# Softmax sums of an attention stage: two engines' halves joined by VectorE and summed one pair of steps later

## The reference, cut to what matters

```python
def mla_attention(q, ckv, kpe, w_kvb, w_o):          # 8 heads; scale = 96 ** -0.5
    ...
    def block(q_blk):
        s = (jnp.einsum('bqhd,bkhd->bhqk', q_blk[..., :QK_NOPE], k_nope)
             + jnp.einsum('bqhr,bkr->bhqk', q_blk[..., QK_NOPE:], kpe))
        p = jax.nn.softmax(s.astype(jnp.float32) * scale, axis=-1).astype(v.dtype)
        return jnp.einsum('bhqk,bkhd->bqhd', p, v)
    ...
    return o @ w_o
```

## Time and profile before

| | us |
|---|---|
| median of 3 runs | 3183.33 |
| lowest and highest | 3180.16 and 3183.79 |
| the profiled execution, its device time | 3184.42 |
| the profiled execution, its span | 3182.6 |

### The profile page before, as it was taken

How to read it: one execution, slowest core, us unless ns; L and a number is a source line. 1 busy time by engine, 2 the same in 40 slices (tenths; PEclk the granted TensorE clock), 3 DMA queues, 4 the chain that set the end, 5 groups by cost and what they waited for, 6 DMA issues and landing times. The chain is left out here.

```text
span 3182.6 us, 43970 instructions
## 1 busy us (share of the span) xinstructions
PE 2928.4 (92%) x16924; PEld 2348.9 (74%) x16924; DVE 1934.8 (61%) x2561; ACT 1084.9 (34%) x1718; POOL 1061.3 (33%) x686
## 2 busy tenths in 40 slices
PE   6999999999789999999999979979954999999993
PEld 2888888888667777777777757768834888888882
DVE  4418393839347777777777746545674555555565
ACT  4411111111344444444444423213422344343434
POOL 0000000000123343444333535421214766666652
PEclk8999999999889999999999999989976999999996
DMA  5312222211540101110110136574414566666667
GB/s 210 109 54 105 76 105 80 105 64 67 177 140 10 27 19 26 25 33 13 27 25 6 60 94 205 173 242 163 158 54 141 184 199 204 202 212 200 207 187 281
DMA packets 139524, 371.26 MB, mean 117 GB/s; under 512 B 20886, under 2 KB 47996, under 8 KB 129116
## 3 DMA queue, kind: packets, MB, share of 16 engines
q1 hardware_dynamic: 99820, 266.47, 25.3%
q0 software_dynamic: 23984, 74.71, 8.3%
q10 hardware_dynamic: 15552, 27.79, 2.5%
HBM read 265.99 MB, written 102.89 MB: 116 GB/s over the span
## 5 line engine op out<-in xcount | busy, mean ns | idle before, releaser
L1160 ACT ACTIVATE at_w<-at_sc 128x512 f32<-128x512 f32 (+1 forms) x592 | 346.3, 591 | 417.8 <-PE at_sc L1235 362.8
L1322 DVE TENSOR_REDUCE at_mpart<-at_mx 128x2 f32<-128x512 f32 x575 | 368.5, 683 | 167.0 <-PE at_mx L1262 166.9
L1210 POOL TENSOR_TENSOR at_part<-at_part,at_w 128x512 f32<-128x512 f32 x224 | 297.4, 1328 | 359.4 <-ACT at_w L1160 356.1
L2479 POOL TENSOR_TENSOR moe_gu_lo<-moe_raw_gu,moe_gu_hi 128x2048 fp32r<-128x2048 f32 x64 | 296.6, 4635 | 121.7 <-ACT moe_gu_hi L2545 121.3
L520 DVE SCALAR_TENSOR_TENSOR fr_r<-fr_r,fr_dw 128x2334 f32<-128x2334 f32 x120 | 318.0, 2650 | 3.9
L377 PE MATMUL fr_po<-hT_hi,fr_w_hi 128*128 128x512 f32 (+1 forms) x800 | 297.1, 371 | 3.1 <-PE fr_po L377 1.9
L377 PE MATMUL fr_po<-hT_hi,fr_w_lo 128*128 128x512 f32 (+1 forms) x800 | 294.7, 368 | 0.0
L377 PE MATMUL fr_po<-hT_lo,fr_w_hi 128*128 128x512 f32 (+1 forms) x800 | 294.6, 368 | 0.0
L1274 PE MATMUL at_acc<-at_w,V 128*64 128x256 f32 (+1 forms) x2368 | 289.7, 384 | 0.0
L2664 DVE TENSOR_TENSOR moe_d_lo<-moe_raw_d,moe_d_hi 128x1024 fp32r<-128x1024 f32 x64 | 184.1, 2876 | 105.3 <-ACT moe_d_hi L2576 105.3
L1349 DVE TENSOR_TENSOR at_part<-at_part,at_w 128x512 f32<-128x512 f32 x224 | 228.9, 1022 | 19.7 <-ACT at_w L1160 6.7
(11 more groups left out here) (391 smaller groups left out, 6800.5 us busy)
## 6 DMA issues: line engine op xcount, KB each, us to landing
moe_raw_gu<-w_gate_up SPq DMA_DIRECT2D x64, 1024.0 KB, 4.8
moe_raw_d<-w_down SPq DMA_DIRECT2D x64, 512.0 KB, 5.2
fr_wm<-w_ada_rows POOLq DMA_DIRECT2D x32, 512.0 KB, 4.1
gates_scratch<-fr_r ACTq DMA_DIRECT2D x64, 256.0 KB, 2.0
mx_gates<-gates_scratch SPq DMA_DIRECT2D x64, 256.0 KB, 3.1
fr_raw<-w_in SPq DMA_DIRECT2D x28, 512.0 KB, 5.1
fr_r<-x POOLq DMA_DIRECT2D x18, 512.0 KB, 4.6
raw<-mixed_scratch SPq DMA_DIRECT2D x9, 1024.0 KB, 6.2
```

The source lines that it names most:

```text
L1160: act.activation(w[:, g % NW, k, 0:n], sc[:, (2 * g + k) % SCB, 0:n], ACT.Exp, scale=SM_SCALE).then_inc(exp_done, 1)
L1210: pool.tensor_tensor(part[:, j % 2, 1, 0:n], before, w[:, g % NW, 1, 0:n], ALU.add).then_inc(add_p, 1)
L1322: dve.tensor_reduce(mpart[:, s, 2 * half:2 * half + 2, c], max_bank(m, half), AX.X, ALU.max).then_inc(red_done, 1)
L2479: pool.tensor_tensor(gu_lo[:, slot], raw_gu[:, slot], gu_hi[:, slot].bitcast(F32), ALU.subtract).then_inc(glo_done, 1)
```

## The change

On every block's end DVE gets one more instruction, `join(j)` (line 1362 of the changed kernel): it adds POOL's partial sum to its own, in place. It waits for both running sums. In DVE's list it stands at the end of the pair in which the block's last `add` is. PE then makes only two products with ones, from the joined sum (`sum_up`), instead of four. They are no longer issued behind the block's last `values` but in the next pair: for b3 between the first `max_products` and the second `scores` of that pair, for all other blocks right ahead of its `values`. ACT's `take_out` moves with them: b3's stands behind the exponentials of the first step of that next pair, those of the others behind the second step's. DVE's `divide` of the last head moves by one pair too. POOL's and SP's lists keep their order.

```diff
+    def ended(g):
+
+        return [block_of(i) for i in (g - 2, g - 1) if i >= 0 and is_last(i)]
...                                                     # scalar (ACT)
-                    if g % 2:
-                        for before in (g - 3, g - 2):
-                            if before >= 0 and is_last(before):
-                                take_out(block_of(before))
+                    for j in ended(g - 2 - g % 2):
+                        if (j % BH == NB - 1) == (g % 2 == 0):
+                            take_out(j)
...                                                     # tensor (PE), in values(g)
-                    if is_last(g):
-                        pe.wait_ge(add_d, ADDS[g + 1])
-                        pe.wait_ge(add_p, ADDS[g + 1])
-                        for k in range(2):
-                            for half in range(2):
-                                mm = pe.matmul(acc[half * DV:(half + 1) * DV, j % 2, 256:256 + n], ones[:],
-                                               part[:, j % 2, k, half * n:(half + 1) * n],
-                                               start=(k == 0), stop=(k == 1), skip_group_check=True)
-                        mm.then_inc(sum_mm, 1)
+
+                def sum_up(j):
+                    n = BLOCKS[j % BH][1] // 2
+                    pe.wait_ge(join_done, j + 1)
+                    for half in range(2):
+                        mm = pe.matmul(acc[half * DV:(half + 1) * DV, j % 2, 256:256 + n], ones[:],
+                                       part[:, j % 2, 0, half * n:(half + 1) * n], start=True, stop=True, skip_group_check=True)
+                    mm.then_inc(sum_mm, 1)
...
+                    for j in ended(g - 2):
+                        if j % BH == NB - 1:
+                            sum_up(j)
                     scores(g + 1)
                     for m in (g + 1 + LA,) if g else range(LA, LA + 2):
                         if m < G:
                             max_products(m)
+                    for j in ended(g - 2):
+                        if j % BH != NB - 1:
+                            sum_up(j)
                     if g:
                         values(g - 2)
                         values(g - 1)
                 values(G - 2)
                 values(G - 1)
+                for j in ended(G - 2) + ended(G):
+                    sum_up(j)
...                                                     # vector (DVE)
+                def join(j):
+                    n, g = BLOCKS[j % BH][1], last_of(j)
+                    dve.wait_ge(add_d, ADDS[g + 1])
+                    dve.wait_ge(add_p, ADDS[g + 1])
+                    dve.tensor_tensor(part[:, j % 2, 0, 0:n], part[:, j % 2, 0, 0:n], part[:, j % 2, 1, 0:n], ALU.add
+                                      ).then_inc(join_done, 1)
...
-                    for i in (g - 2, g - 1):
-                        if i >= PER * (H - 1) and is_last(i):
-                            divide(block_of(i))
+                    for j in ended(g):
+                        join(j)
+                    for j in ended(g - 2):
+                        if j >= BH * (H - 1):
+                            divide(j)
```

More of the change, by code:

```diff
@@ L1012, in attention_phase @@
         s_mm, exp_done, pv_mm, sum_mm = (p.sem(n) for n in ("s_mm", "exp_done", "pv_mm", "sum_mm"))
-        add_d, add_p = p.sem("add_d"), p.sem("add_p")
+        add_d, add_p, join_done = p.sem("add_d"), p.sem("add_p"), p.sem("join_done")
         m_mm, red_done = p.sem("m_mm"), p.sem("red_done")
@@ L1176, in _ @@
                         act.activation(weight(i)[0], wraw[:], ACT.Copy).then_inc(w_hi_done, 1)
-                for g in (G - 2, G - 1):
-                    if is_last(g):
-                        take_out(block_of(g))
             @block.gpsimd
@@ L1396, in _ @@
                 add(G - 1)
-                for i in (G - 2, G - 1):
-                    if is_last(i):
-                        divide(block_of(i))
+                for j in ended(G):
+                    join(j)
+                for j in ended(G - 2) + ended(G):
+                    divide(j)
 def mix_phase(nc, t, raw, c_ld, m_ld, wc_hi, wc_lo, wo_hi, wo_lo, w1_hi, w1_lo):
```

## The result

| | before | changed |
|---|---|---|
| median, us | 3182.57 (4 runs, 3180.16 to 3183.79) | 3217.84 (4 runs, 3214.88 to 3225.58) |
| profiled execution, device time and span | 3184.42, 3182.6 | 3218.96, 3217.2 |

The ratio is 1.0116, 95% interval 1.0098 to 1.0133. The change costs 35.3 us. I had forecast +17.2 and a top of 3216. The direction was right, the size was not.

A forecast was written before the change was run, and what follows sets the result against it. PE was taken to bound the attention, with the keys' DMA chain barely on its path. -16.1 + 1 + 0 + 23.3 + 9 = +17.2 us gave 3200.5 us, own range 3191 to 3214, eight-in-ten range 3185 to 3216.

The forecast's parts named there:

- the chain: Behind a head's end: prompt block's take-out, sums' read-back, keys' DMA, split; 9.11 us (even), 12.42 (odd), barely on the path.
- Part 1: At the block ends in the attention, half of PE's products with ones go: -16.1 us.
- Parts 2 and 3: In the attention, products moving to the next pair: +1 us (bounds 0 and 3); 40 joins on DVE: 0.
- third rival: Joins in the attention delay PE as well, half of them on the path, adding 22 us: 3223 us; chance 0.06.
- The fourth: Rival: at the block ends, halving the products with ones saves nothing: 3217 us; chance 0.03.
- Part 4: At six heads' ends the prompt block's take-out and the next keys' DMA come later: +23.3 us (21.8 to 29.2).
- Part 5: PE's clock falls to half rate behind five of six waits at heads' ends: +9 us (bounds +2 and +15).
- The first and second rivals: At heads' ends, first: keys' delay absorbed, 3168 us, chance 0.11; second: stalls about two thirds, a draw, 3183, chance 0.10.

The follow-up runs named there:

- early keys: Loads of the next head's keys moved ahead of the stores of b3 and the prompt block: kernel before 3174.66 us (0.9968), changed kernel 3173.54 us (0.9959).
- the version of 48 memsets: Changed kernel with the keys loaded early and 48 idle memsets on DVE in the attention: 3170.36 us, ratio 0.9947 to the kernel before.
- join only: Kernel before with the join and two products, issued at the old place without the move: 3191.92 us, ratio 1.0026.
- defer only: Changed kernel without the join: four products as before, issued in the next pair: 3224.68 us, ratio 1.0125 to the kernel before.
- the second pair of traces: Both kernels run again unchanged: before 3184.07 us (0.9997), changed 3222.47 us (1.0116).
- the kernel with the memsets at the end: Kernel before with 80 idle memsets behind DVE's last instruction of the program: 3186.74 us, ratio 0.9997.

## Why the forecast missed

- **What bounds the kernel, and the chain.** Right. It was read from two small rows of waits and one timeline, and the early keys confirm it: the chain cost 8 to 10 us before and 42.9 after.
- **Part 1, -16.1.** Measured -15.8 with the changed order. With early keys the whole change, parts 1 to 3 together, is -13.7, against -15.1 in the forecast; compared with the version of 48 memsets, whose attention is 907.4, it is -12.2.
- **Parts 2 and 3, +1 and 0.** No wait for a join in the changed kernel, and DVE's wait for maxima products fell by only 8.6 us, not 25 to 40. The third rival (joins delay PE) is out here; join only shows that it was a real danger, and that the move averts it. The fourth gave 3217, next to the measured 3217.84. That is a coincidence: defer only shows the saving that it denied.
- **Part 4, +23.3.** Measured +23.1, with three waits near 7.3 us and three near 2.5 as worked out. The lower bound of 21.8 does not follow from the terms given, which make 17.7 + 5.0 = 22.7; the total's lower end would be 3192 and the range hardly another.
- **Part 5, +9.** All six waits went with a fall, not five. The measured price is 13.0 - 3.0 = +10.0, inside the bounds. The Trainium skill ("TensorE: Matmul & The Clock Gate", What's actually happening) has the half rate as the default, which activity has to release. The forecast took from this that every one of the six waits is followed by a fall, and +11.4. That count is the forecast's own step, since the sentence does not say which waits are long enough. It came out right for the six here, and not for the four before; the odd ones at 1.7 us each were cheaper than the 2.4 taken.
- **The first and second rivals** had part of the delay absorbed. The chain kept its 9.06 us; nothing was absorbed.
- **The step that failed** is the term that the sum put at nothing: the other phases. "The change touches none of them" was taken to mean that they stay as long as they were, and the forecast laid the attention's +17.2 on the profiled execution's time as if the rest stood still. The attention has 19.4 of the 35.3 us (20.9 in the second pair of traces), near what was forecast. Outside it, the experts' loop pays 7.7 us, because 80 instructions of DVE stand ahead of it. With these in the sum it would have been 3200.5 + 7.7 = 3208, inside the range, and still 10 us short.
- **What stays open** is the rest, some 7 to 8 us of the medians. The front is 931.8 to 935.1 us in eight of the fourteen traces and 939.4 to 941.9 in six. All six have the longer list of DVE, but so have three of the eight, and the kernel with the memsets at the end has the long front and a ratio of 0.9997. That the length of the program bears on the front is not shown. Half a microsecond lies outside the span: device time exceeds it by 1.8 us in each run of before, by 1.8 to 3.3 in those of the changed kernel. Nor is it shown why DVE's jump back takes twice as long at one place of the list as at another; only that it goes with the place, at 0, 80 and 128 instructions more.

## What to carry to other kernels

When an operation is put off, follow what stands behind it in every queue down to the next load: here a take-out six microseconds later moved a DMA chain of 9 us whole, and 16 us of saved products were paid with 33 us of waits and half clock. Move the load out of the chain first; then the same change gains. And compare the phases that were not edited: where which of two engines comes first at a port hangs on less than 0.2 us, instructions added far ahead of a loop can flip the order, here by the time of the jump back. So a change of a few tenths of a per cent is judged by stages, with idle instructions of the same number as a control.

## What the hardware showed that I had not expected

- 80 idle memsets of 59 ns each cost the phase they stood in nothing and a phase that begins 1000 us later 6 to 8 us; the same 80 behind that phase cost nothing. What changed in that phase at first hand was the jump back of a loop on DVE, 0.13 to 0.14 us or 0.26 to 0.29.
- A wait of PE of only 2.5 us was followed each time by a stretch at the clock of 1.2 GHz (0.57 granted over 4.0 us). For shorter ones the length did not decide: in the first trace of before, waits of 1.4 to 1.8 us were followed by none and one of 2.02 us by over 6 us of it; in the second, two of 1.89 us by 3.4 us of it each, and one of 2.16 us by none.
- An indirect DMA's issue on POOL took 0.96 us when it began 0.03 us ahead of a DVE operation with two SBUF inputs, and 1.93 us when it began 0.13 us behind it.
